# Neighbourhood attention as one list of groups, and one left sum of the MLP's last quarter moved

## The reference, cut to what matters

```python
h = modulate(rms_norm(x_lat, g_attn[l]), sh1, sc1)
gl, mq, mk, mv, nq, nk, nv = mixer_proj(h, *proj_w)     # nq, nk: rms_norm per head of 64
...
y_mla = blocked_attention(mq, [mk_c, mk], [mv_c, mv])
y_na = neighborhood_attention(nq, nk, nv, nk_c, nv_c, rpb[l])
x_lat = x_lat + gt1 * gated_merge(gl, y_mla, y_na, w_mla_o[l], w_na_o[l], w_out[l])
h2 = modulate(rms_norm(x_lat, g_mlp[l]), sh2, sc2)
x_lat = x_lat + gt2 * (jnp.square(jax.nn.relu(h2 @ w_ff1[l])) @ w_ff2[l])
```

## Time and profile before

| | |
|---|---|
| median of three runs | 4365.98 us (4363.13 to 4372.34) |
| profiled execution | 4366.17 us |
| its span, first to last instruction | 4364.3 us |
| mean granted TensorE clock | 0.927 |
| TensorE busy | 3779.7 us, 87% of the span |
| VectorE busy | 1760.8 us, 40% |
| ScalarE busy | 753.6 us, 17% |

### The profile page before, as it was taken

How to read it: one execution, slowest core, us unless ns; L and a number is a source line. 1 busy time by engine, 2 the same in 40 slices (tenths; PEclk the granted TensorE clock), 3 DMA queues, 4 the chain that set the end, 5 groups by cost and what they waited for, 6 DMA issues and landing times. The chain is left out here.

```text
span 4364.3 us, 38500 instructions
## 1 busy us (share of the span) xinstructions
PE 3779.7 (87%) x14796; PEld 2148.8 (49%) x14796; DVE 1760.8 (40%) x3066; ACT 753.6 (17%) x1671; POOL 169.9 (4%) x373
## 2 busy tenths in 40 slices
PE   7987776899388999999728698999998699999998
PEld 3653763344244445555314445458743354447843
DVE  0128734345313211111233546355445355445545
ACT  0212101111022211000112424110001253211000
POOL 1000000000100000000020300000000300000000
PEclk9988876999599899999968899999998899999999
DMA  7442001322276678788732110122221301032221
GB/s 290 164 154 107 1 5 49 135 96 94 91 289 233 256 290 321 314 343 316 262 140 76 51 58 20 68 106 77 77 99 49 111 20 58 13 122 77 78 77 58
DMA packets 197610, 572.54 MB, mean 131 GB/s; under 512 B 23844, under 2 KB 35412, under 8 KB 184424
## 3 DMA queue, kind: packets, MB, share of 16 engines
q1 hardware_dynamic: 180856, 524.07, 32.3%
q0 software_dynamic: 7184, 23.91, 1.5%
q10 hardware_dynamic: 9392, 22.12, 1.4%
HBM read 539.39 MB, written 30.69 MB: 131 GB/s over the span
## 5 line engine op out<-in xcount | busy, mean ns | idle before, releaser
L342 PE MATMUL ps<-out_sums 128*128 128x256 f32 (+1 forms) x1152 | 333.6, 451 | 2.3 <-issue 2.3
L342 PE MATMUL ps<-mixers_xT,ring 128*128 128x512 f32 (+2 forms) x864 | 293.2, 499 | 0.9 <-PEq L272 0.9
L342 PEld LDWEIGHTS ps<-out_sums 128*128 128x128 f32 x1152 | 219.2, 190 | 113.8 <-issue 94.3
L342 PE MATMUL ps<-ring,mixers_xT 128*128 128x512 f32 (+3 forms) x736 | 257.7, 508 | 10.1 <-DVE ab_qk L336 6.1
L342 PEld LDWEIGHTS ps<-mixers_xT,ring 128*128 128x128 f32 (+1 forms) x864 | 161.6, 188 | 127.7 <-issue 116.4
L342 PEld LDWEIGHTS ps<-ring,mixers_xT 128*128 128x128 f32 x736 | 139.1, 203 | 125.1 <-issue 111.1
L342 PE MATMUL ps<-ring,layers_hT 128*128 128x512 f32 x416 | 185.7, 604 | 15.3 <-PEq L272 13.1
L2205 PE MATMUL ps<-ring,moe_xgT 128*64 128x512 f32 x416 | 186.5, 606 | 3.2 <-issue 2.3
L2206 PE MATMUL ps<-ring,moe_xgT 128*64 128x512 f32 x416 | 183.7, 598 | 0.0
L342 PE MATMUL ps<-ring,out_hidden 128*128 128x512 f32 x352 | 153.4, 592 | 0.0
L342 PEld LDWEIGHTS ps<-ring,layers_hT 128*128 128x128 f32 x416 | 79.9, 194 | 116.8 <-issue 112.7
(11 more groups left out here) (868 smaller groups left out, 6171.1 us busy)
## 6 DMA issues: line engine op xcount, KB each, us to landing
ring<-in_w_ff SPq DMA_DIRECT2D x44, 2048.0 KB, 12.8
ring<-in_w_in SPq DMA_DIRECT2D x40, 2048.0 KB, 12.9
ring<-in_e_up SPq DMA_DIRECT2D x27, 2048.0 KB, 9.9
ring<-in_e_gate SPq DMA_DIRECT2D x25, 2048.0 KB, 15.4
ring<-in_e_down SPq DMA_DIRECT2D x25, 2048.0 KB, 8.9
ring<-in_w_ada SPq DMA_DIRECT2D x24, 2048.0 KB, 11.5
ring<-in_w_out SPq DMA_DIRECT2D x8, 2048.0 KB, 11.5
deep_ring_more<-in_e_gate SPq DMA_DIRECT2D x8, 2048.0 KB, 13.9
```

What stands on the lines that cost most here:

```text
L342: last = pe.matmul(out, lhsT, rhs, start=(j == 0), stop=(j == len(pairs) - 1))
```

## The change

Neighbourhood attention becomes one call of `products`, with `PAIRED_BANKS` throughout, and its order is written out.

- The four bias groups stand after "2", "5" and "6". The parts of `seven` come in the order "1", "2", "5", "6", "3", "7", "4".
- The norms are made in four pairs of row blocks, which share two buffers of squares, and each pair follows soon after the part that completes it.
- Value products 0 and 1 stand ahead of the transposes, product 2 after the second step of the attention's list, product 3 after the third. Products 0 and 2 are moved by ScalarE, 1 and 3 by VectorE (the other way round before).
- The gain is the first group on VectorE, and the two context loads are the first on ScalarE (SP issued them before).
- k, the reversed rows and p1 lie in `heads`, which later holds the turned probabilities, and the squares lie in the attention's score rows.

```diff
+        context = [group(None, lambda act, _, link: act.dma_start(
+                       kT[:, :, T:T + CTX], M.ctx_nk[l].rearrange("p (k n) -> p k n", k=4)), "s", dma=True),
+                   ...
-            vs = row_groups(M, t0 + 2, 0, NA_W, hT, lambda t: v[:, t, :])
+        vs = row_groups(M, t0 + 2, 0, NA_W, hT, lambda t: v[:, t, :], on="sv")
...
-            q_work, q_made = rms_groups(M, si, "nq", q, TT, MH, HD, made=[(g,) for g in qs])
-            k_work, k_made = rms_groups(M, si, "nk", k, TT, MH, HD, made=[(g,) for g in ks])
+        work, made = {}, {}
+        for i, r in ((0, 0), (1, 0), (1, 1), (0, 1)):
+            work[i, r], made[i, r] = rms_groups(M, st, f"n{'qk'[i]}{r}", (q, k)[i][:, 2 * r:2 * r + 2, :], 2, MH, HD,
+                                                made=[(ends[2 * r + t, i],) for t in range(2)], share=squares)
...
-            products(M, f"na_p{l}",
-                     sum(qk, []) + spread(vs, spread(q_work + k_work, bias)) + [gain] + turned,
-                     tiles=3, extra={"sync": small, "late": landed, "gpsimd": masks})
+        gs = context + [gain] + qk[0] + qk[1] + bias[0:1] + qk[2] + bias[1:2] + qk[3] + bias[2:4] + qk[5] + work[0, 0]
+        gs += qk[4] + work[1, 0] + qk[6] + work[1, 1] + vs[0:1] + work[0, 1] + vs[1:2] + turned
...
-        with Stage(nc, f"na_att{l}") as sa:
-            products(M, f"na_a{l}", sum(attend(M, sa, f"na{l}", quads, 2, BANK, 5), []), pools=PAIRED_BANKS)
+        order = attend(M, st, f"na{l}", quads, 2, BANK, 5, (S_rows, PT))
+        order[0][0].needs += tuple(context + turned)
+        order[0][0].after += tuple(bias)
+        order[4][-1].needs += tuple(vs)
+        gs += order[0] + order[1] + vs[2:3] + order[2] + vs[3:4] + sum(order[3:], [])
+        products(M, f"na_p{l}", gs, tiles=3, extra={"sync": small, "gpsimd": prepare}, pools=PAIRED_BANKS)
```

```diff
+    spare = hidden[:, 0:2, :].rearrange("p k n -> p (k n)").rearrange("p (k n) -> p k n", k=half)
+    def last_left(after):
+        a11, a12, a21, a22 = a(parts - 1)
+        return group(None, lambda dve, _, link: dve.tensor_tensor(spare, a12, S[1], ALU.subtract), "v", after=after)
...
         gs += [s3, r3]
+        if ends:
+            s4 = last_left((s2,))
+            gs.append(s4)
         both("6", S[1], R[1], (s2, r2), u2, lambda x: (now["1", x], now["5", x], before["3", x]))
-        s4, r4 = left(k, 4, (now["6", 1],)), right(k, 4, (now["6", 1],))
-        gs += [s4, r4]
+        if not ends:
+            s4 = left(k, 4, (now["6", 1],))
+            gs.append(s4)
+        r4 = right(k, 4, (now["6", 1],))
+        gs.append(r4)
         if ends:
-            both("3", S[1], b22, (s4,), c12, lambda x: (now["6", x],))
+            both("3", spare, b22, (s4,), c12, lambda x: (now["6", x],))
```

More of the change, by code:

```diff
@@ L2896, in latent_attention, with bias_groups @@
             products(M, f"mla_p{l}", sum(attend(M, sa, f"mla{l}", quads, 1, T + CTX, TA), []), pools=PAIRED_BANKS)
-def bias_groups(M, st, l, table, flip, flip_made):
-    rev = st.sb("rev", [P, MH // 2, 2, 2 * P])
+def bias_groups(M, st, l, rev, table, flip, flip_made):
     arrived = [st.sig[f"bias_in{x}"] for x in range(MH // 2)]
@@ new lines, in neighbourhood_attention @@
+        heads = st.sb("heads", [P, 2 * 2 * 5 * 2 * P])
+        S_rows = st.sb("S", [P, 3, 2, BANK])
+        gains = st.sb("gains", [P, 2])
+        size = TT * NA_W
+        q = yT[:, :, :].rearrange("p k n -> p (k n)").rearrange("p (t n) -> p t n", t=TT)
+        k = heads[:, 0:size].rearrange("p (t n) -> p t n", t=TT)
+        rev = heads[:, size:2 * size].rearrange("p (x h n) -> p x h n", x=MH // 2, h=2)
+        p1 = [heads[:, 2 * size + x * BANK:2 * size + (x + 1) * BANK] for x in range(2)]
@@ new lines, in neighbourhood_attention, with prepare @@
+        PT = heads[:, :].rearrange("p (q h c n) -> p q h c n", q=2, h=2, c=5)
+        squares = Squares([S_rows[:, 0, x, :] for x in range(2)])
+        def prepare(pool):
+            link = Chain(pool, st.sig["masks"])
+            link(pool.memset(zero[:, :], 0.0))
+            link(pool.memset(flip[:, :], 0.0))
+            link(pool.affine_select(out=flip[:, :], in_=flip[:, :], compare_op=ALU.not_equal, fill=1.0,
+                                    base=1 - P, pattern=[[1, P]], channel_multiplier=1))
+            pool.sem_inc(st.sig["flip_made"], 1)
+            load_bias(pool)
@@ new lines, in small @@
+        def small(sp):
+            for i, name in enumerate(("g_na_q_2", "g_na_k_2")):
+                for p0 in (0, HD):
+                    sp.dma_start(gains[p0:p0 + HD, i:i + 1], A[name][l].rearrange("n -> n ()")
+                                 ).then_inc(st.sig["small"], 16)
+        context = [group(None, lambda act, _, link: act.dma_start(
+                       kT[:, :, T:T + CTX], M.ctx_nk[l].rearrange("p (k n) -> p k n", k=4)), "s", dma=True),
+                   group(None, lambda act, _, link: act.dma_start(
+                       v[:, TT:TA, :], M.ctx_nv[l].rearrange("p (t n) -> p t n", t=TC)), "s", dma=True)]
@@ new lines, in scale_gain @@
+        def scale_gain(eng, _, link):
+            eng.wait_ge(st.sig["small"], 64)
+            return eng.tensor_scalar(gains[:, 0:1], gains[:, 0:1], HD ** -0.5, None, ALU.mult)
+        gain = group(None, scale_gain, "v")
+        t0 = M.weights.taken
+        R = two_sums([qT[:, :, :].rearrange("p k n -> p (k n)"), v[:, 0:TT, :].rearrange("p t n -> p (t n)")])
+        qk, ends, _ = seven(M, t0, t0 + 1, row_quarters(hT), four_sums(sums), None, R, p1,
+                            lambda x, i, j: (q, k)[j][:, 2 * i + x, :])
@@ new lines, in edges, with inner @@
+        def edges(pe, bank, w=M.weights.view(t0 + 2)):
+            for j in range(DK):
+                for p0, c0 in ((0, 0), (HD, T - HD)):
+                    last = pe.matmul(bank[p0:p0 + HD, :], hT[:, j, c0:c0 + HD], w[:, j, :],
+                                     start=j == 0, stop=j == DK - 1)
+            return last
+        def inner(pe, bank, t, w=M.weights.view(t0 + 2)):
+            return matmuls(pe, bank, [(hT[:, j, t * P - HD:(t + 1) * P - HD], w[:, j, :]) for j in range(DK)])
@@ new lines, in neighbourhood_attention @@
+        vs = row_groups(M, t0 + 2, 0, NA_W, hT, lambda t: v[:, t, :], on="sv")
+        vs[0].pe = edges
+        for t in range(1, TT):
+            vs[t].pe = lambda pe, bank, t=t: inner(pe, bank, t)
+        bias, load_bias = bias_groups(M, st, l, rev, table, flip, st.sig["flip_made"])
+        work, made = {}, {}
+        for i, r in ((0, 0), (1, 0), (1, 1), (0, 1)):
+            work[i, r], made[i, r] = rms_groups(M, st, f"n{'qk'[i]}{r}", (q, k)[i][:, 2 * r:2 * r + 2, :], 2, MH, HD,
+                                                made=[(ends[2 * r + t, i],) for t in range(2)], share=squares)
@@ new lines, in neighbourhood_attention @@
+        turned = []
+        for i, (x, xT) in enumerate(((q, qT), (k, kT))):
+            turned += transposes(
+                M, lambda t, j, x=x: x[:, t, j * P:(j + 1) * P], None, TT, 4,
+                evac=lambda eng, bank, link, j, a, n, xT=xT, i=i: scaled(
+                    eng, xT[:, j, a * P:(a + n) * P], bank, gains[:, i:i + 1]),
+                needs=[(g, gain) for g in made[i, 0] + made[i, 1]])
+        gs = context + [gain] + qk[0] + qk[1] + bias[0:1] + qk[2] + bias[1:2] + qk[3] + bias[2:4] + qk[5] + work[0, 0]
@@ L3457, in layer_output @@
             nxt = layers[l + 1]
-            xn2 = flat[:, 0:TILE].rearrange("p (t d) -> p t d", d=D)
-            squares = Squares([flat[:, TILE + i * D:TILE + (i + 1) * D] for i in range(2)])
+            xn2 = flat[:, 2 * BANK:2 * BANK + TILE].rearrange("p (t d) -> p t d", d=D)
+            squares = Squares([flat[:, 2 * BANK + TILE + i * D:2 * BANK + TILE + (i + 1) * D] for i in range(2)])
             work, scaled_ = halves_normed(M, st, "next", x, ready, xn2, squares)
```

## The result

The changed kernel takes 4335.02 us (median of 4 runs, 4330.77 to 4338.24) against 4367.33 for the kernel before (4 runs, 4363.13 to 4372.34): ratio 0.9925, 95% interval 0.9908 to 0.9942. Forecast was 4335.9. The profiled executions took 4338.24 and 4366.17 us, 27.9 apart, with spans of 4336.5 and 4364.3; the forecast was 30.1 less.

The account below looks back on a forecast made before the run. TensorE was taken as the engine to follow, with time won only where it waits or runs slow. Neighbourhood stages 16.9 us plus MLP ends 13.2 made 30.1 us, giving 4335.9 us; range 4328 to 4350.

Parts of the forecast that it names:

- The wait and the clock at the transposes: Ahead of the query transposes, waits of 4.52 and 4.53 us go; full clock saves 1.38 and 2.07 us more.
- The seam: Between the two lists, a 1.03 us wait, mostly for scalar's last move: no gain taken, bounds 0 and 0.3 us.
- The softmax's start: Value products 2 and 3 cover start-up waits of 3.01 us, one of 0.8 stays: gain 2.2 us a layer.
- The hold by the gain: At the stage's start, the gain heading vector's list holds vector about 4.5 us until its small transfers land.
- no cost: The gain's hold on vector costs nothing, since R1, wanted only by product "5", has 7 us of slack.
- The banks: Input part with 4 PSUM banks instead of 8: cost taken as 0, by distance between groups and moves.
- a wait per group: Every input group waits about 1.0 us for its move: 26 groups, two layers, 52 us, 4388 us; chance 3%.
- The MLP: Left sum computed ahead of product "6"; vector late next, so gains are 7.3 us (layer 0) and 5.9 (layer 1).
- the rival by which all waits turn into time: All waits go and vector does not bound the MLP's end: 34 us won, 4332 us; chance 5%.
- the third rival: The MLP sum gives nothing, its stall returning at "7" or the bank: 16.9 us alone, 4349 us; chance 5%.
- the banks' rival: Four banks take back what the neighbourhood stage gains: 13.2 us alone, 4352.8 us; chance 7%.

Follow-up runs that it names:

- experiment 3: Changed kernel with value products 2 and 3 back ahead of the transposes: 4345.88 us, ratio 0.9955 to the kernel before.
- experiment 7: Changed kernel with the two context loads on scalar's queue behind the first two products instead of at the head: 4336.3 us in one run.
- experiment 6: Changed kernel with the gain behind the moves of product 2 on vector instead of first: one run of 4338.22 us.
- Experiment 4: Kernel before with its neighbourhood attention input list rotating through 4 banks instead of 8: 4366.92 us, ratio 1.0001.
- Experiment 5: Changed kernel with 2 banks instead of 4 outside the scores in the neighbourhood list: 4366.14 us, ratio 1.0002 to the kernel before.
- experiment 2: Kernel before with the neighbourhood's edit alone, the MLP as before: 4350.73 us, ratio 0.9964.
- experiment 1: Kernel before with the MLP's edit alone, neighbourhood attention as before: 4356.12 us, ratio 0.9971.
- experiment 9: Changed kernel with value product 0 right ahead of the transposes, product 1 behind them, and each MLP's last right-hand sum on GpSimd: 4335.74 us.

## Why the prediction was right, and where its terms were off

The waits that it named went, and vector set the end of the MLP as it said. The terms, one by one:

**The wait and the clock at the transposes.** The 4.52 and 4.53 us went as forecast. The pair of norms that decides is scaled at 2621.1 and the first transpose runs at 2623.85, 2.7 us of cover against 2.5. The clock's share was sized too small: I took 2.10 us for sixteen transposes at full speed from the earlier trace rows, but that row still held some of the slow clock. They take 1.91. So 5.58 - 3.82 = 1.76 us went in layer 0 and 6.27 - 3.82 = 2.45 in layer 1, 0.38 more than forecast in each.

Which part of the edit took the 4.5 us away is not shown: no run moved the gain alone. VectorE's timeline of the kernel before, layer 0, shows what stood for what.

```profile
2620.14 0.69 DVE L2538 TENSOR_TENSOR layers_yT<-layers_yT,na_in_nq_rs 128x512 f32<-128x512 f32 x1
...
2636.20 1.81 DVE L2920 TENSOR_TENSOR na_table<-ps,na_mask 128x192 f32<-128x192 f32 x6
2637.92 0.14 DVE L3006 TENSOR_SCALAR na_in_gains<-na_in_gains 128x1 f32<-128x1 f32 x1
```

The query transposes need the norms of q and the gain, and the last norm of q was scaled by 2620.83; TensorE's work ahead of them ended at 2633.59. They stood for the gain alone. The key transposes need the last norm of k, which was scaled by 2636.28, and vector's share of the moves that the first scores wait for stood behind the last bias table, until 2638.01. So the gain at the head of vector's list would by itself have let the query transposes start, and the earlier norms and tables serve the key transposes and the first scores. How the 4.5 us split between the two is open.

**The seam.** I took no gain between bounds of 0 and 0.3; it gave 0.21 (1.03 to 0.82). The waiting is, as forecast, for the last moves. The table load ends at 2629.5, before the first exponentials at 2631.07, and costs nothing.

**The softmax's start.** Start-up waits of 3.01 us became one of 0.75 in the third turn: 2.26 against 2.2 forecast, and experiment 3 gives 2.39 back when the products go (3.78 in layer 1, with slow clock). In layer 1 one later wait is 0.19 longer, which leaves 2.09.

With this layer 0 is 4.52 + 1.76 + 0.21 + 2.26 = 8.75 of 8.91, layer 1 is 4.53 + 2.45 + 0.21 + 2.09 = 9.28 of 9.39; the rest of 0.1 to 0.2 is small change between rows.

**The hold by the gain.** Forecast about 4.5 us with 7 of slack; it was 8.0, since the context loads went to another queue and landed beside the gains. With those loads behind the first two products it is 4.3 (experiment 7), as reckoned. The step "no cost" held all the same (experiment 6), with less slack than I gave it: in VectorE's timeline of the changed kernel right-hand sum 1, which product "5" reads, runs right behind the gain,

```profile
2566.27 2.29 DVE L1863 TENSOR_TENSOR na_qT<-ring 128x2048 f32<-128x2048 f32 x1
```

and ends at 2568.56, and product "5" begins at 2572.86: 4.3 us of slack. Sum 2 ends at 2570.89, but product "6" reads it, at 2580.59. The 2 us that the expectation of experiment 6 names are from sum 2 to product "5", which does not need it.

**The banks.** Experiment 4 decides what the trace before could not: eight to four costs nothing in this list, ratio 1.0001 with bounds of 0.1%. The Trainium skill's page "Perfetto Trace Analysis", section "Matmul Optimizations", asks that all eight be used. For eight against four this list does not bear that out (ratio 1.0001); for four against two the stages show a price. Experiment 5 shows the same mechanism biting one step on: with two, 18.0 and 16.1 us of waits and slow clock a stage, 34 in all. That is two thirds of the 52 us that the rival of "a wait per group" reckoned, and 20.1 of the 34 lie in the input part. The changed list itself was never run with eight banks; what speaks for four there is that no wait for a bank stands in its input part.

**The MLP.** From the start of right-hand sum 3 to the first move of "7": before, 3288.05 (line 3126) to 3311.77, 23.72 us; after, 3282.85 to 3299.24, 16.39. That is 7.33, forecast 7.3. In layer 1 22.36 became 16.39, 5.97 against 5.9. Vector was late next, as forecast, and so the rival by which all waits turn into time fell. The two layers differ by 1.36 us, as do the slow matmuls behind the old wait, 9.91 and 8.55. These differ between executions too (experiment 2), and so does what this edit wins.

**The sum.** 18.3 + 13.3 = 31.6 us against 30.1, most of the difference in the clock and the seam. The two profiled spans differ by 27.8, because unchanged work ahead of the first neighbourhood stage ended 4.2 us later in this execution (2558.20 against 2554.04); the medians differ by 32.3, 25 to 40 by the interval. How near the forecast came is in part the luck of which execution was profiled: with the old list layer 0 took 151.69 us in the trace that the forecast was read from, and 153.86 in those of experiments 1 and 4, against which the same edit wins 11.1 us and not 8.9.

**The range.** Its upper end, 4350, is not what its parts make: the third rival's 4349 and 6 us are 4355, beyond the 4352.8 of the banks' rival that was to lie outside; the lower parts make 4329, not 4328. The measured 4335.02 lies far from both ends.

## What to carry to other kernels

Cover a wait with work that needs nothing of what it waits for, in the length that the wait has: two products moved behind the start of the softmax won 2.4 us in one stage and 3.8 in the other (experiment 3), and one moved from where cover was in surplus to the seam won 0.9 more. When TensorE's wait falls away, look for the engine that is late next before the gain is booked: at the MLP's end vector kept 1.6 of the 14.9 us that TensorE's list alone would have given. Ask which of several things that stand ahead of a late instruction its user needs: in the trace before, the query transposes stood for the gain alone, and the change moves norms and tables too, without a run that tells their shares apart. And a short wait is worth more than its own length where slow matmuls follow it, but by an amount that differs from run to run: take the full-speed duration from a row far from any wait.

## What the runs showed of the hardware

**GpSimd and vector stood still for each other.** In experiment 9 vector's instruction with two inputs in SBUF stood until GpSimd's sum was done; in experiment 6 GpSimd's selection stood until vector's sum was done (1.83 us, as in the kernel before, against 0.29 alone). The Trainium skill's page "SBUF — State Buffer", section "Who interferes with whom", says that a VectorE instruction with two SBUF inputs and a GpSimd instruction that reads SBUF share a port, and that whichever starts second is blocked until the first is done. Both traces agree, one for each order. The sum itself took 4.67 us on GpSimd, its first 0.3 beside an instruction of vector, and 2.28 on vector.

**Small transfers landed later with big ones issued beside them.** Transfers of 0.2 KB landed 2.3 and 2.5 us after issue, and 3.7 and 6.0 with two loads of 512 KB issued at the same time from another queue (experiment 7). In the kernel before, where the same two loads stood behind them on their own queue, they landed after 2.3. A transfer that an engine waits for is better issued ahead of bulk that nobody waits for yet.

**The start of the softmax costs clock only sometimes.** In experiment 3 the same start-up waits left the transposes (line 488, eight of them) at 1.06 us in layer 0 and at 1.91 in layer 1.
